# An expert stage on one core: experts written out in place of a loop, a token gather that serves two experts, 14 weight buffers in place of 12, and overflow blocks without a scatter of their own

## The chip, the cores and the metric

The kernel runs on one NeuronCore of a Trainium2 chip. The metric is the device time of one execution in microseconds. Before the change three runs took 2330.51, 2333.76 and 2336.15 us, median 2333.76.

## The reference

Two transformer blocks in fp32 for 256 tokens of width 1024. The part that the change touches is the mixture of experts in the first block:

```
logits = xt @ w_router + b_router                 # 256 x 32
top_logits, top_idx = top_k(logits, 4)            # 4 of 32 experts for each token
top_w = softmax(top_logits)
# for each expert e, over the tokens that chose it:
gate, up = split(xb @ w_gu[e] + b_gu[e], 2)       # w_gu[e]: 1024 x 2048
gate = minimum(gate, 7.0); up = clip(up, -7.0, 7.0)
act  = (up + 1) * (gate * sigmoid(1.702 * gate))
yb   = act @ w_dn[e] + b_dn[e]                    # w_dn[e]: 1024 x 1024
y[token] += yb * top_w
```

Each of the 32 experts has 12 MB of fp32 weights, 384 MB in all, read once. Before this stage comes a token mixer with its own projections, behind it pooling, a gated delta rule and two feed-forward layers; the change doesn't touch them.

## The kernel before

**Units.** All weights come in units of 1 MB, 128 partitions by 8 KB, issued in order by SyncE (SP). `ring` holds 10 of them; `area` is eleven slabs of 8 KB per partition for everything else. An expert is 12 units: 8 for gate and up (unit kt holds rows 128*kt and following of `w_gu`), 4 for the down projection (order `DN_ORDER`). In the expert stage unit u of every expert has the fixed buffer `eslot[u]` (line 184): the ring's 10 and the slabs 9 and 10. SP waits for `w_used`, which TensorE raises with the last matmul that reads a unit, and refills it (lines 506 to 515, one hardware loop over experts 1 to 31). TensorE waits for `w_full[u]` (line 986).

**Blocks.** Tokens of an expert are handled in blocks of 64 slots. An expert with over 64 tokens has overflow blocks (up to three) that run before its last block (`b` = 0) and read the same weights, without giving buffers back. `experts` (line 466) is the control flow of TensorE, VectorE and ScalarE alike: a hardware loop over the experts, in which the expert's token count is loaded into a register, then an inner hardware loop over b = 1 to 3 with an `If`: the overflow block, or an `Else` that only raises the step semaphore by the number of skipped steps (line 477). The three engines keep in step by counting semaphores (`Steps`, line 435): a wait names an expert, a block and a step.

**A last block on TensorE** (line 1066): bias matmuls for gate and up (`gate_and_up`, line 967, recorded at 971), 32 gate and up matmuls with 64 stationary columns (979), the scatter of the *previous* block's output into four PSUM banks (1023, recorded at 1027), the gather of the next expert's tokens (`gather`, 956, recorded at 960: one-hot matmuls of h2_tok with `slots`, 64 columns wide), two transposes each of the activation (994), the transpose of the spread matrix (1002), 16 down matmuls (1016). An fp32 matmul that isn't a transpose leaves two records and two weight loads. In one block there are 146 matmul records and 146 loads, 292.

**An overflow block** (line 1053): it waits until ScalarE has finished with the block before (`AC.started`), gathers its own tokens, waits for VectorE's copy of them, does gate and up, spread transpose, activation transposes and down, waits for ScalarE's y copy, and scatters its own output. It has buffers of its own for spread, spread_T and y (`spread_o`, `spread_T_o`, `y_blk_o`; `spread_o` lies in slab 5).

**VectorE** makes the one-hot masks (`find_slots`, line 1853, for the next expert; `find_spread`, 1860), the limits of gate and up (1872, 1873), the products (1877, 1881), the copies of the gathered tokens (1865) and of the transposed activation (1886). **ScalarE** does the sigmoid (1394), the copy of the transposed spread (1396) and, at a block's end, the copy of y out of PSUM (1401). Ahead of the loop TensorE gathers for expert 0 and starts the four output banks with the down bias (1049); VectorE makes the masks of expert 0 (1892) and copies g2 (1904) and the tokens (1906).

After the last expert the late stream of weights uses four ring buffers, which SP refills as expert 31 frees them (line 490), and ScalarE splits each unit in two parts (210).

## Time and profile before

| | |
|---|---|
| median of 3 runs | 2333.76 us (2330.51 to 2336.15) |
| the profiled execution | 2335.09 us |
| its span, first to last instruction | 2333.0 us |
| mean granted TensorE clock | 0.947 of 2.4 GHz |
| PE busy | 2102.5 us, 90% |
| PE weight loads | 1346.1 us, 58% |
| DVE busy | 854.8 us, 37% |
| ACT busy | 433.0 us, 19% |
| moved by DMA | 578.65 MB, mean 248 GB/s |

How to read it: PE is TensorE's matmuls and PEld its weight loads, DVE is VectorE, ACT ScalarE, SP SyncE. Times are us from the span's start unless marked ns. A line number is that of the kernel before. "Idle before" is the time in which the engine did nothing ahead of an instruction, with what ended it; "issue" is time for which the profile shows no cause, and PEq, ACTq and DVEq are sequencers. The DMA share is that of 16 DMA engines together; packets that overlap a little make a full load read as slightly over 100%. The expert stage begins near 400 us and ends near 1460 us.

### The profile page before, as it was taken

The numbers are of one execution on the slowest core, as the hardware profiler recorded it, in microseconds if no ns is written. First come the engines' busy times: TensorE is split into PE (matmuls) and PEld (weight loads), VectorE is DVE, ScalarE is ACT, GpSimd is POOL, SyncE is SP. The second block draws the span as 40 slices with busy tenths as digits, with TensorE's granted clock in tenths as the row PEclk, the third lists the DMA queues.
The fourth block names the chain that finished last, engine by engine and source line by source line (L and its number), as shares of the span: only waits on it lengthen the run. The fifth ranks groups of instructions, "written<-read, shape, count | busy, mean of one in ns | idle before, by whom it ended". The sixth has DMA issues, their size and how long they took to land. (4 is left out here: it accounts for less than half of the span.)

```text
span 2333.0 us, 30897 instructions
## 1 busy us (share of the span) xinstructions
PE 2102.5 (90%) x11317; PEld 1346.1 (58%) x11318; DVE 854.8 (37%) x1404; ACT 433.0 (19%) x503; POOL 61.8 (3%) x126
## 2 busy tenths in 40 slices
PE   5999996999999998999998989599988877769997
PEld 3768784434444443444443434389868865657986
DVE  1295335111111111111111111646557674544654
ACT  1011101001011000001100000135324422113541
POOL 2000002000000000000000000100000000000000
PEclk9999896999999999999999999799999986979999
DMA  9487322949999997999997948245554300124552
GB/s 362 159 285 277 121 108 92 401 192 419 422 422 422 422 422 329 368 422 422 422 422 317 385 194 356 100 156 186 189 166 142 108 1 1 55 65 138 181 198 73
DMA packets 142572, 578.65 MB, mean 248 GB/s; under 512 B 10521, under 2 KB 12041, under 8 KB 93259
## 3 DMA queue, kind: packets, MB, share of 16 engines
q1 hardware_dynamic: 135824, 563.12, 62.2%
q0 software_dynamic: 3552, 12.61, 1.6%
q10 hardware_dynamic: 3131, 1.98, 0.3%
q8 instruction: 50, 0.82, 0.1%
q14 instruction: 15, 0.12, 0.0%
HBM read 576.62 MB, written 1.05 MB: 248 GB/s over the span
## 5 line engine op out<-in xcount | busy, mean ns | idle before, releaser
L979 PE MATMUL bank<-ring,area 128*64 128x512 f32 x2304 | 505.6, 596 | 1.8 <-DMA ring<-in_w_gu 1.8
L979 PEld LDWEIGHTS bank<-ring,area 128*64 128x64 f32 x2304 | 167.3, 138 | 320.2 <-issue 306.8
L213 DVE TENSOR_TENSOR ring_r<-ring,ring_r 128x2048 fp32r<-128x2048 f32 x92 | 210.9, 2292 | 210.4 <-ACT ring_r L210 209.5
L709 PE MATMUL bank<-area,ring 128*128 128x256 f32 x1024 | 232.1, 390 | 9.9 <-issue 8.0
L709 PEld LDWEIGHTS bank<-area,ring 128*128 128x128 f32 x1024 | 200.3, 196 | 43.0 <-issue 12.1
L210 ACT ACTIVATE ring_r<-ring 128x2048 fp32r<-128x2048 f32 x92 | 175.8, 1912 | 234.6 <-PE bank L746 209.8
L1872 DVE TENSOR_SCALAR area<-bank 128x512 f32<-128x512 f32 x36 | 24.9, 691 | 505.1 <-PE bank L979 505.1
L743 PE MATMUL bank<-area_r,ring_r 128*128 128x256 f32 x704 | 201.4, 286 | 2.2 <-DVE area_r L1764 2.2
L745 PE MATMUL bank<-area_r,ring_r 128*128 128x256 f32 x704 | 200.1, 284 | 0.0
L746 PE MATMUL bank<-area_r,ring_r 128*128 128x256 f32 x704 | 200.0, 284 | 0.0
L743 PE MATMUL bank<-ring_r,area_r 128*128 128x512 f32 x384 | 153.2, 399 | 1.7 <-DVE area_r L1764 1.7
L960 PEld LDWEIGHTS bank<-area 128*128 128x128 f32 x1184 | 135.0, 192 | 31.8 <-DVE area L1873 24.3
L745 PE MATMUL bank<-ring_r,area_r 128*128 128x512 f32 x384 | 151.9, 396 | 0.0
L746 PE MATMUL bank<-ring_r,area_r 128*128 128x512 f32 x384 | 151.8, 395 | 0.0
L960 PE MATMUL bank<-area 128*128 128x64 f32 x1184 | 140.0, 276 | 3.8 <-ACT area L1401 2.8
L743 PEld LDWEIGHTS bank<-area_r,ring_r 128*128 128x128 f32 x704 | 136.1, 193 | 3.1 <-issue 3.1
L745 PEld LDWEIGHTS bank<-area_r,ring_r 128*128 128x128 f32 x704 | 136.1, 193 | 0.5 <-issue 0.5
L746 PEld LDWEIGHTS bank<-area_r,ring_r 128*128 128x128 f32 x704 | 136.1, 193 | 0.0
L1016 PE MATMUL bank<-ring,area 128*64 128x512 f32 x576 | 132.5, 602 | 0.6 <-DVE area L1886 0.5
L1016 PE MATMUL bank<-area 128*64 128x512 f32 x576 | 129.7, 592 | 0.0
L1394 ACT ACTIVATE area<-area 128x512 f32<-128x512 f32 x36 | 22.7, 629 | 456.9 <-DVE area L1872 456.9
L1853 DVE TENSOR_SCALAR area<-slot_row,place 128x64 f32<-128x64 f32 (+1 forms) x72 | 15.0, 251 | 234.6 <-PEq L477 231.5
(294 smaller groups left out, 1993.7 us busy)
## 6 DMA issues: line engine op xcount, KB each, us to landing
ring<-in_w_gu SPq DMA_DIRECT2D x256, 1024.0 KB, 15.8
ring<-in_w_dn SPq DMA_DIRECT2D x64, 1024.0 KB, 12.7
area<-in_w_dn SPq DMA_DIRECT2D x64, 1024.0 KB, 14.2
ring<-in_mlp_w SPq DMA_DIRECT2D x64, 1024.0 KB, 5.4
ring<-in_w_mod SPq DMA_DIRECT2D x24, 1024.0 KB, 7.5
ring<-in_w_in SPq DMA_DIRECT2D x24, 1024.0 KB, 9.1
ring<-in_gdn_w_in SPq DMA_DIRECT2D x16, 1024.0 KB, 5.4
ring<-in_ple_gate_w SPq DMA_DIRECT2D x8, 1024.0 KB, 7.5
```

Of the source, the lines that this page charges most:

```text
L210: nc.scalar.activation(unit_high(i), raw, ACT.Copy).then_inc(w_high, 1)
L213: nc.vector.tensor_tensor(unit_low(i), raw, unit_high(i), ALU.subtract).then_inc(w_split, 1)
L709: ins = mm(bank(g)[:, m * S:(m + 1) * S], u[k // UK][:, k % UK, c:c + P], xT[:, k, :], start=k == 0, stop=k == ND - 1)
L743: ins = mm(out_, a_[0], b_[0], start=start, stop=False)
L745: mm(out_, a_[0], b_[1], start=False, stop=False)
L746: return mm(out_, a_[1], b_[0], start=False, stop=stop)
L960: ins = mm(bX[:, d * BLK:(d + 1) * BLK], h2_tok[:, t, d * P:(d + 1) * P], s_[:, t, :], start=t == 0, stop=t == NT - 1)
L979: ins = mm(bk[hf * BLK:(hf + 1) * BLK, :], x[:, kt, :], eslot[kt][:, c:c + BANK], start=False, stop=kt == ND - 1)
L1016: ins = mm(bT[hf * BLK:(hf + 1) * BLK, :], actT[:, 2 * i + k, fh * BLK:(fh + 1) * BLK], eslot[u][:, c:c + BANK], start=n == 0 and k == 0, ...
L1394: f(g_sig, g_min, ACT.Sigmoid, scale=SWIGLU).then_inc(moe_act, 1)
L1853: step(v.tensor_scalar(dst[:, t, :], row, place[:, t, bass.ds(e, 1)], None, ALU.is_equal))
L1872: step(v.tensor_scalar(g_min, banks[5][:, :], LIMIT, None, ALU.min))
```

## The change

- The loop over experts is a Python loop: 32 copies of the inner loop and of the last block, on TensorE, VectorE, ScalarE and SP. The inner loop over overflow blocks stays a hardware loop in each copy. Waits in last blocks are on constants.
- `gather_pair` takes the place of `gather` for last blocks: the tokens of a pair of experts (128 columns) are gathered together, half of the features (4 of 8 slices) in each of the two blocks of the pair before. `slots` and `xg` have two halves; masks are made three experts ahead. The first pair is gathered ahead of the stage in two banks. Overflow blocks keep `gather`.
- 14 buffers: the ring's 10, slabs 9, 10, 5 and 8. Unit n of the 384 goes to buffer n mod 14.
- An overflow block no longer scatters its own output: like a last block it scatters that of the block before it, between gate/up and the transposes, and leaves its own to the next. It uses the shared spread, spread_T and y buffers, and waits for the y copy of the block before only there. The bias matmuls stand ahead of the wait for the token copy.

```
-        eslot = [ring[:, u, :, :].rearrange("p k n -> p (k n)") if u < RING else a(9 + u - RING)
-                 for u in range(NU)]
+        eslot = [ring[:, u, :, :].rearrange("p k n -> p (k n)") for u in range(RING)] + [a(9), a(10), a(5), a(8)]
+        ER = len(eslot)
+        def expert_slot(e, u):
+            return (NU * e + u) % ER
...
         def experts(eng, steps, overflow, last_block):
-            with eng.Fori(0, NE) as e:
-                n_tok = eng.value_load(counts[0:1, bass.ds(e, 1)], min_val=0, max_val=S)
+            for e in range(NE):
+                n_tok = eng.value_load(counts[0:1, e:e + 1], min_val=0, max_val=S)
                 with eng.Fori(1, NBLK) as b:
                     with eng.If(n_tok - b * BLK > 0):
                         overflow((e, b))
...
-            with sp.Fori(1, NE) as e:
+            for e in range(NE):
                 for u in range(NU):
-                    sp.wait_ge(w_used, e * NU + (PRE - NU + u + 1))
-                    sp.dma_start(eslot[u], expert_source(u, e)).then_inc(w_full[u], 16)
+                    n, s = NU * e + u, expert_slot(e, u)
+                    if n >= ER:
+                        sp.wait_ge(w_used, PRE + n - ER + 1)
+                    elif n < RING:
+                        sp.wait_ge(w_used, PRE - RING + n + 1)
+                    elif n == RING:
+                        sp.wait_ge(areas_free, 1)
+                    elif n == RING + 2:
+                        sp.wait_ge(w_used, PRE)
+                    elif n == RING + 3:
+                        full(sp, G("g2_bc", 1))
+                    sp.dma_start(eslot[s], expert_source(u, e)).then_inc(w_full[s], 16)
...
+            def gather_pair(bk, p, dh):
+                for d in range(UK):
+                    for t in range(NT):
+                        ins = mm(bk[:, d * P:(d + 1) * P], h2_tok[:, t, (UK * dh + d) * P:(UK * dh + d + 1) * P],
+                                 slots[:, p, t, :], start=t == 0, stop=t == NT - 1)
+                step(ins)
...
             def overflow(w):
                 DV.did(pe, w, "slots1")
-                AC.started(pe, w)
+                AC.started(pe, w, less=1)
                 gather(slots_o)
+                gate_up_bias()
                 DV.did(pe, w, "tokens")
-                gate_and_up(w[0], xg_o, False)
-                spread_transposed(w, spread_o)
+                gate_and_up(w, xg_o, False)
+                AC.started(pe, w)
+                scatter(spread_T, y_blk)
+                spread_transposed(w, spread)
                 activation_T(w, 0, bG)
                 activation_T(w, 1, bU)
                 down(w, False)
-                AC.did(pe, w, "down")
-                scatter(spread_T_o, y_blk_o)
...
             def last_block(w):
-                e = w[0]
+                pair, j = w[0] // 2, w[0] % 2
                 DV.started(pe, w)
-                gate_and_up(e, xg, True)
+                gate_up_bias()
+                gate_and_up(w, xg[:, pair % 2, :, j * BLK:(j + 1) * BLK], True)
                 AC.started(pe, w)
                 scatter(spread_T, y_blk).then_inc(w_used, 1)
                 DV.did(pe, w, "next_slots1")
-                gather(slots)
+                gather_pair(bX, (pair + 1) % 2, j)
...
-            for t in range(NT):
-                n[0] += 1
-                v.tensor_scalar(slots[:, t, :], slot_row[:, 0, 0, :], place[:, t, 0:1], None, ALU.is_equal)\
-                    .then_inc(dve_step, 1)
+            for e in range(3):
+                for t in range(NT):
+                    n[0] += 1
+                    v.tensor_scalar(slots[:, e // 2, t, e % 2 * BLK:(e % 2 + 1) * BLK], slot_row[:, 0, 0, :],
+                                    place[:, t, e:e + 1], None, ALU.is_equal).then_inc(dve_step, 1)
```

## Rows read from the trace of the kernel before

**Rows 1.** Timeline: first gate matmul, y copies of ScalarE (start, us, engine, line)

```profile
402.95 16.54 PE L979 MATMUL bank<-ring,area 128*64 128x512 f32 x64
...
492.38 0.60 ACT L1401 ACTIVATE area<-bank 128x512 f32<-128x512 f32 x1 [9.12 <-PE bank L1016]
...
553.47 0.60 ACT L1401 ACTIVATE area<-bank 128x512 f32<-128x512 f32 x1 [6.64 <-PE bank L1016]
...
838.12 0.60 ACT L1401 ACTIVATE area<-bank 128x512 f32<-128x512 f32 x1 [6.64 <-PE bank L1016]
...
897.77 0.60 ACT L1401 ACTIVATE area<-bank 128x512 f32<-128x512 f32 x1 [6.64 <-PE bank L1016]
...
1247.12 0.60 ACT L1401 ACTIVATE area<-bank 128x512 f32<-128x512 f32 x1 [6.64 <-PE bank L1016]
...
1277.50 0.60 ACT L1401 ACTIVATE area<-bank 128x512 f32<-128x512 f32 x1 [9.12 <-PE bank L1016]
...
1459.69 0.60 ACT L1401 ACTIVATE area<-bank 128x512 f32<-128x512 f32 x1 [6.64 <-PE bank L1016]
```

**Rows 2.** Windows: length, five engines' busy (x), clock, DMA share, GB/s

```profile
450.00:500.00 50.00, 43.34 (x234) 19.66 (x236) 8.40 (x23) 5.05 (x7) 0.00 (x0) 1.00 0.42 175
550.00:600.00 50.00, 49.33 (x254) 20.09 (x250) 8.79 (x22) 5.40 (x7) 0.00 (x0) 1.00 1.01 422
```

**Rows 3.** Who waited for whom, loads of TensorE, stage (us, times, longest)

```profile
PEld bank L979 <- DMA ring<-in_w_gu: 7.2, 8, 1.4
```

**Rows 4.** The timeline of one plain block and the next one's start

```profile
712.10 3.79 PE L960 MATMUL bank<-area 128*128 128x64 f32 x32
712.41 0.76 DVE L1881 SCALAR_TENSOR_TENSOR area<-area 128x256 f32<-128x256 f32 x2
...
724.25 0.60 ACT L1401 ACTIVATE area<-bank 128x512 f32<-128x512 f32 x1 [6.64 <-PE bank L1016]
...
724.83 5.75 PE L979 MATMUL bank<-ring,area 128*64 128x512 f32 x26
...
727.38 1.28 ACT L1394 ACT_TABLE_LOAD   x1 [2.54 <-ACTq L477]
```

**Rows 5.** The timeline of TensorE behind the stage, matmuls 128x128 by 128

```profile
1480.06 0.39 PE L1096 MATMUL bank<-apad,area 128*128 128x128 f32 x2
1480.28 0.39 PE L1098 MATMUL bank<-apad,area 128*128 128x128 f32 x2
```

**Rows 6.** The timeline of TensorE, overflow block of expert 2 and the block after

```profile
462.66 3.79 PE L960 MATMUL bank<-area 128*128 128x64 f32 x32 [0.70 <-ACT area L1401]
...
484.23 0.84 PE L994 MATMUL bank<-ident,area 128*128 128x128 f32 x4 [2.28 <-DVE area L1881]
...
497.15 3.18 PE L979 MATMUL bank<-ring,area 128*64 128x512 f32 x14
```

**Rows 7.** The timeline ahead of the stage

```profile
390.68 0.42 DVE L1892 TENSOR_SCALAR area<-slot_row,place 128x64 f32<-128x64 f32 x2
...
402.09 0.19 PEld L971 LDWEIGHTS bank<-area,expert_sel 96*64 96x64 bf16 x4 [4.24 <-DVE area L1853]
```

**Rows 8.** Queue q8: whole page, then 410 to 1450; a window between two packets

```profile
q8 instruction: 50, 0.82, 0.1%
...
q8 instruction: 1, 0.02, 0.0%
...
1561.17:1576.40 15.23, 15.23 (x130) 1.00 0.64 199
```

**Rows 9.** Queues at 162.3:163.6, 163.6:164.9, 164.9:166.2 (packets, MB, share of 16 engines)

```profile
q1 hardware_dynamic: 264, 0.51, 106.6%
...
q1 hardware_dynamic: 237, 0.49, 99.2%
q8 instruction: 1, 0.02, 5.3%
...
q1 hardware_dynamic: 258, 0.50, 104.6%
```

More of the change, by code:

```diff
@@ L323, in empties @@
             ins.then_inc(bank_free[g % BANKS], 1)
-        w_full = [sem(f"w_full{u}") for u in range(NU)]
+        w_full = [sem(f"w_full{u}") for u in range(ER)]
         w_used = sem("w_used")
@@ L961, in gather, with gate_up_bias @@
                                  start=t == 0, stop=t == NT - 1)
-                        if d == 0 and t == 0:
-                            first = ins
                 step(ins)
-                return first
-            def gate_and_up(e, x, last):
+            def gate_up_bias():
                 for part, bk in ((0, bG), (1, bU)):
@@ L1016, in down @@
                             ins = mm(bT[hf * BLK:(hf + 1) * BLK, :], actT[:, 2 * i + k, fh * BLK:(fh + 1) * BLK],
[L1017 removed]
+                                     block_u[:, c:c + BANK], start=n == 0 and k == 0, stop=n == 3 and k == 1)
                     if last:
@@ L1037, in _ @@
             pe.wait_ge(moe_dve, 1)
+            assert all(G("g2_bc", q) % BANKS not in (4, 6) for q in range(2)) and G("gateT") % BANKS not in (4, 6)
+            for dh in range(2):
+                gather_pair((bX, bU)[dh], 0, dh)
+            emptied(pe, G("gateT"))
             for q in range(2):
-                if G("g2_bc", q) % BANKS == 4:
-                    emptied(pe, G("g2_bc", q))
-            gather(slots)
-            emptied(pe, G("gateT"))
+                emptied(pe, G("g2_bc", q))
             pe.wait_ge(route_ready, 4)
             pe.wait_ge(bgu_ready, 1)
-            for q in range(2):
-                emptied(pe, G("g2_bc", q))
             for i in range(4):
@@ L1072, in last_block @@
                 DV.did(pe, w, "next_slots1")
-                gather(slots)
+                gather_pair(bX, (pair + 1) % 2, j)
                 activation_T(w, 0, bG)
```

90 lines of the change are left out of this document (46 added, 44 removed).

## The prediction

> **What bounds the kernel now.** I read the page's slices first, then windows of the expert stage, then the marks that each block leaves on ScalarE, then single blocks, then who waits for what, and last the instruction queue. The profiled execution took 2335.09 us with a span of 2333.0 us, 1.3 us over the median of 2333.76. The expert stage is 45% of it: from the first gate matmul at 402.95 us to the last y copy at 1459.69 us, 1056.7 us [rows 1]. The transfers run at 422 GB/s with all 16 engines full where no overflow block is near (550 to 600), and at 175 GB/s around the first one, where every buffer is full [rows 2]. TensorE's clock is 1.00 in the full stretches, the upper level of 2.4 GHz.
>
> An expert's 12 units are 12.58 MB: at 422 GB/s 29.8 us, 2.486 us for a unit. TensorE needs less: the marks of ten experts in a row (553.47 to 838.12) are 28.46 us apart, and only then come two at 29.8 (to 897.77), the pace of the transfers [rows 1]. So TensorE eats up the lead of 12 buffers at 1.4 us an expert; just as it is gone the next overflow block comes, in which TensorE frees no buffer for 30 us. Waits of the gate matmuls for weights come to only 7.2 us on the load side [rows 3]. **The two limits lie 5% apart**: whatever is saved on TensorE in the long runs (experts 2 to 15 and 16 to 26) can only reach the transfers' limit. Overflow blocks belong to experts 2, 16, 27 and 29: a mark with an idle of 9 us or more ends one.
>
> **Part by part.**
>
> *Gather for two.* Today one block gathers 64 slots with 32 matmul records in 3.79 us, between the scatter and the transposes, on the path [rows 4]. That is 0.118 us a record though only 64 columns move. The new half gather has 16 records with 128 moving columns. Such matmuls stand in L1096 and L1098: a pair starts every 0.22 us, 0.11 us for one [rows 5]. 16 of them are 1.8 to 1.9 us. The saving lies between nothing and 2.0 us; I take 1.95, as those rows are the same shape back to back. Does the gate chain still hide? SCALAR_TENSOR_TENSOR ends at 713.17; scatter and short gather end at 714.0, so the transposes don't wait; the token copy, 128x512 as before, follows the gather by the same 0.3 us. TensorE's pace becomes 28.46 - 1.95 = **26.5 us**.
>
> *Overflow blocks.* Before, one waits 0.70 us for the y copy before it gathers [rows 6]; and the block after it starts its gate 4.8 us after the down projection (own scatter 1.99, y copy, masks, turn of the loop) where a plain one needs 0.6: 492.38 to 497.15 against 724.25 to 724.83 [rows 1, 4, 6]. Now the scatter lies where the gate chain left TensorE idle for 2.28 us. The bias matmuls go under the token copy (0.6). The block takes 29.7 in place of 30.4, the next loses 4.2.
>
> *14 buffers.* The two more are filled before the stage, when the queue is idle, and let the transfers run 5.0 us longer at each stop. SP's queue is passed in order: unit 12 needs only the last earlier use, unit 13 the copy of g2, which VectorE makes right behind the masks of [rows 7], 10 us before the stage; nothing urgent stands behind them. At the other end the late stream's first four units take the buffers of expert 31's units 6 to 9 rather than 0 to 3, some 12 us later; the last comes free 4 us before the end and is needed after it, so I put nothing on it. If that cover fails, ScalarE's first splits slip by up to 2 us.
>
> *Head.* Four more mask instructions of 0.21 us stand before the first gather: +0.8 us, on the path [rows 7].
>
> *Waits on constants.* ScalarE's turn between blocks idles 2.54 us before its table load [rows 4]; TensorE's turn is hidden but for 0.2 us behind queued matmuls. Constants spare a few register steps of it; nothing.
>
> *Written out 32 times.* This is the part with a price that one must look for. A block body is 292 TensorE records, and the loop has two bodies. In the whole stage the instruction queue q8 fetches one packet of 16 KB: the loop stays resident. Outside it fetches one per 130 matmuls with their 130 loads, 50 in all [rows 8]. Written out, an expert is 260 + 292 records (the overflow body is passed over but lies there), 552, and with control some 575: 2.25 packets each, 70 more in the stage. What does one cost? In three windows of 1.3 us at full load the weights' queue q1 has 106.6%, 99.2% and 104.6% of 16 engines, and in the middle one q8 has 5.3%: 0.053 x 16 x 1.3 = 1.10 us of an engine, taken from q1 one for one [rows 9]. A unit is spread over all 16 engines and has landed when the last has its share. If q8 always sits on **one and the same engine**, that engine serves 29.83 + 2.25 x 1.10 to 1.2 = 32.4 us per expert and everyone waits for it: a unit takes 2.70 us. If the packets spread, or slip between, it stays 2.486. No row of the kernel before decides this. All 50 packets come one at a time from one queue of one sequencer; q1 has its packets on 16 engines at once. I take one engine.
>
> **The sum**, in stretches between the marks (before; then with a unit at 2.70; then at 2.486):
> - Experts 0 and 1 and the overflow of 2: 89.4; 89.4 - 3.9 + 0.8 - 0.7 = 85.6; 85.6.
> - Experts 2 to 15: 405.4. All 14 buffers are full, 168 - 14 = 154 units come, plus 4 us to start after the standstill and 2 us to use the last: 421.8; 388.8. TensorE alone would need 371.
> - Overflow of 16 and experts 16 to 26: 349.4. The overflow waits for its own weights, 31.5; 29.7. Some 11.8 units come meanwhile, 120.2 are left, plus 2: 326.8; 300.6. So 358.3; 330.3.
> - Overflow of 27: 30.4; 31.5; 29.7.
> - Experts 27 to 31 with the overflow of 29: 182.2; 5 x 26.5 + 29.7 = 162.2; 162.2.
>
> Together 1056.7; 1059.4; 996.6. So +2.7 us with one engine, -60 without. The 23 us saved in the short stretches and at the overflow blocks are given back in the two long ones.
>
> To both comes the jump over the overflow body, 303 instructions, more than one packet: where its target isn't there TensorE stands still. In the long runs the transfers hide it; 11 jumps are unhidden. Price: at least the packet's 1.1 us, at most the 4.2 us that the loads idle at the loop's first entry [rows 7]; with a quarter to all of them late this is 3 to 46 us. I take 2.7 us on a quarter: 7 us.
>
> Forecast: 2335.1 + 2.7 + 7 - 1.3 (to the median) = **2344 us**.
>
> **Rivals.**
> - *The fetches cost nothing* (the other side: faster). 2335.1 - 60 + 7 - 1.3 = 2281 us. Point of decision: fetch time per expert on the fullest engine; below 1.5 us an expert (a unit at 2.61) the kernel gains over 15 us, at 2.4 it is level. For it: that a queue may use many engines, as q1 does. Against: the one-for-one loss at full load. The Trainium skill (Runtime: NRT & Kernel Launch, section Instruction fetch mechanics) says that crossing a fetch boundary is "mostly hidden"; by that rule this rival is what happens. It speaks of the sequencer, and of that the rows agree: no matmul gap stands at a packet in straight code.
> - *Every jump is late.* TensorE's pace is 29.5 instead of 26.5 where it counts, 11 x 3 = 33 us more in place of 7: 2370 us. For it: the body passed over is longer than a packet, and the 4.24 us of idle at the loop's entry. Against: ScalarE's plain turn also takes 2.54 us, so most of that can be control alone. The same section says that a taken branch out of the resident window stalls for a fetch, and that kernels prefer full unrolling for it; here the branch stays when the loop goes, so the rule would turn against this change.
> - *The half gather is no shorter* (bound of that term). Pace 28.46: 14 us more with one engine, 2358 us; 36 more with spread fetches, 2318.
>
> **How the numbers follow.** One engine pays 0.58 (2344, own range 2328 to 2362), fetches free 0.29 (2270 to 2318), late jumps 0.13. The range 2282 to 2362 leaves out the lower part of the free case and most of the late jumps. About 0.2%, 4.7 us, is what a measurement can tell. The first case lies 10 us over the kernel before with some 10 us of doubt: 0.08 of it faster, 0.20 same. So faster 0.34, same 0.12, slower 0.54.
>
> **What would show it.** Marks in experts 3 to 6 at 26.5 us (gather right), at 28.5 (not). Marks in 9 to 15 at 32.4 (one engine) or 29.8 (free), and GB/s there 388 or 422. q8: about 70 packets more. q1's share of 16 engines there well below 100% with waits of TensorE for the ring (one engine), or at 101% (free). Idle of 1 to 4 us before L971's loads on some experts: late jumps. Overflow blocks 29.7 us. I am wrong altogether if the late stage after 1460 moves by more than 2 us by itself.

## The result and the profile after

The changed kernel takes **2315.57 us** (median of 4 runs, 2312.82 to 2318.56) against 2333.99 for the kernel before beside it: ratio 0.9918, 95% interval 0.9901 to 0.9936. It is 18 us faster, 0.8%. The forecast was 2344 us, slower: the sign is wrong, the range of 2282 to 2362 us holds the time.

The profiled execution took 2318.56 us, span 2316.8 us. First the marks (the y copy that ScalarE makes at a block's end, now L1424) that answer to [rows 1]: ends of expert 1, of 2's overflow block, of experts 2, 3, 4 and 15, of 16's overflow block, of 26, of 27's overflow block and of 31.

```profile
460.70 0.60 ACT L1424 ACTIVATE area<-bank 128x512 f32<-128x512 f32 x1 [6.71 <-PE bank L1038]
489.90 0.60 ACT L1424 ACTIVATE area<-bank 128x512 f32<-128x512 f32 x1 [8.09 <-PE bank L1038]
517.98 0.60 ACT L1424 ACTIVATE area<-bank 128x512 f32<-128x512 f32 x1 [6.71 <-PE bank L1038]
544.35 0.60 ACT L1424 ACTIVATE area<-bank 128x512 f32<-128x512 f32 x1 [6.71 <-PE bank L1038]
579.00 0.60 ACT L1424 ACTIVATE area<-bank 128x512 f32<-128x512 f32 x1 [6.71 <-PE bank L1038]
...
895.24 0.60 ACT L1424 ACTIVATE area<-bank 128x512 f32<-128x512 f32 x1 [6.71 <-PE bank L1038]
924.44 0.60 ACT L1424 ACTIVATE area<-bank 128x512 f32<-128x512 f32 x1 [8.09 <-PE bank L1038]
...
1238.42 0.60 ACT L1424 ACTIVATE area<-bank 128x512 f32<-128x512 f32 x1 [6.71 <-PE bank L1038]
1267.62 0.60 ACT L1424 ACTIVATE area<-bank 128x512 f32<-128x512 f32 x1 [8.09 <-PE bank L1038]
...
1442.95 0.60 ACT L1424 ACTIVATE area<-bank 128x512 f32<-128x512 f32 x1 [6.71 <-PE bank L1038]
```

The expert stage, from the first gate matmul at 403.56 to the last mark, is 1039.4 us (before 1056.7). What follows the last mark is the same: 873.9 against 873.3 us. A clean block takes 544.35 - 517.98 = 26.37 us, an overflow block 29.20. But every fourth expert takes 33.4 to 34.7 us (579.00 - 544.35 = 34.65), and the one after it often 28 to 30. The timeline of TensorE at the first matmuls of blocks (bias, L989; experts 3, 4, 5, 6, 7 and 8) shows where that goes; the bracket is the idle time before them:

```profile
517.76 0.60 PE L989 MATMUL bank<-area,expert_sel 96*64 96x512 bf16 x4
549.55 1.06 PE L989 MATMUL bank<-area,expert_sel 96*64 96x512 bf16 x4 [5.25 <-DVE area L1876]
581.00 0.62 PE L989 MATMUL bank<-area,expert_sel 96*64 96x512 bf16 x4 [2.05 <-DVE area L1876]
609.02 0.62 PE L989 MATMUL bank<-area,expert_sel 96*64 96x512 bf16 x4 [1.46 <-DVE area L1876]
635.41 0.60 PE L989 MATMUL bank<-area,expert_sel 96*64 96x512 bf16 x4
667.33 1.06 PE L989 MATMUL bank<-area,expert_sel 96*64 96x512 bf16 x4 [5.39 <-DVE area L1876]
```

The releaser that is named, VectorE's mask, is a consequence and not the cause. At expert 4 that mask starts at 549.26 us, after 11.77 us in which VectorE waited for TensorE's sequencer (PEq L486, the count that TensorE raises behind its jump):

```profile
549.26 0.42 DVE L1876 TENSOR_SCALAR area<-slot_row,place 128x64 f32<-128x64 f32 x2 [11.77 <-PEq L486]
```

VectorE had raised the count for which TensorE's bias matmuls wait by 540.04. After 5.25 us of idle the four bias matmuls take 1.06 us in place of 0.62, and the next window has a lower clock. Windows at the stall (length, busy time of PE, PEld, DVE, ACT, POOL, granted clock, DMA share, GB/s):

```profile
540.00:550.00 10.00, 4.75 (x26) 1.38 (x22) 0.74 (x4) 0.60 (x1) 0.00 (x0) 0.92 1.01 416
550.00:560.00 10.00, 10.00 (x38) 3.26 (x36) 0.18 (x1) 0.00 (x0) 0.00 (x0) 0.73 0.98 398
560.00:570.00 10.00, 10.00 (x52) 4.10 (x49) 2.74 (x5) 0.63 (x1) 0.00 (x0) 1.00 0.97 393
```

So one stall costs its 5.25 us and 3 more, in which TensorE runs partly at 1.2 GHz. Against a plain 26.37 us (28.04 behind an overflow block) the blocks lose 70 us in all by the marks, 46 of them in six blocks that take 33.4 us or more.

Who waited for whom in the stage, on TensorE and its loads; no line of TensorE or of its loads names weights:

```profile
PEld bank L989 <- DVE area L1876: 73.5, 31, 6.3
PE bank L989 <- DVE area L1876: 55.0, 19, 5.4
```

And the queues in 500 to 900, where the transfers are full in both kernels, first before, then after (packets, MB, share of 16 engines):

```profile
q1 hardware_dynamic: 23003, 167.60, 100.9%
```

```profile
q1 hardware_dynamic: 22943, 167.05, 100.6%
q8 instruction: 31, 0.51, 0.5%
```

31 packets of code came in these 400 us, and q1 moved 0.55 MB less: just about the code's own bytes. **One engine always held up by q8 would have cost 31 x 1.1 = 34 us of 400, some 14 MB.** The reason that I gave for a unit of 2.70 us is refuted by this alone.

### The profile page after: what moved, and what is told of

It is laid out like the page before. It is cut to its first block and busy times, and to the rows that moved or that the text cites. A ratio compares the mean times of both kernels' runs of the same rounds, so it can differ in the third digit from the quotient of the medians.

```text
span 2316.8 us, 27597 instructions
## 1 busy us (share of the span) xinstructions
PE 2059.3 (89%) x10805; PEld 1299.8 (56%) x10805; DVE 856.3 (37%) x1408; ACT 388.4 (17%) x467; POOL 61.7 (3%) x126
## 5 line engine op out<-in xcount | busy, mean ns | idle before, releaser
L1000 PE MATMUL bank<-ring,area 128*64 128x512 f32 x1632 | 370.5, 609 | 0.7 <-issue 0.5
L1000 PEld LDWEIGHTS bank<-ring,area 128*64 128x64 f32 x1632 | 124.4, 141 | 232.8 <-issue 229.4
L1038 PE MATMUL bank<-ring,area 128*64 128x512 f32 x848 | 188.6, 595 | 0.5 <-DVE area L1909 0.5
L1000 PE MATMUL bank<-area 128*64 128x512 f32 x672 | 152.4, 603 | 2.0 <-issue 1.3
L1038 PEld LDWEIGHTS bank<-ring,area 128*64 128x64 f32 x848 | 58.5, 137 | 112.3 <-issue 104.8
L1000 PEld LDWEIGHTS bank<-area 128*64 128x64 f32 x672 | 50.9, 139 | 94.6 <-issue 91.0
```

The costliest lines, as they stand in the source:

```text
L1000: ins = mm(bk[hf * BLK:(hf + 1) * BLK, :], x[:, kt, :], block_u[:, c:c + BANK], start=False, stop=kt == ND - 1)
L1038: ins = mm(bT[hf * BLK:(hf + 1) * BLK, :], actT[:, 2 * i + k, fh * BLK:(fh + 1) * BLK], block_u[:, c:c + BANK], start=n == 0 and k == 0, s ...
```

## The experiments

Theories. **J**: TensorE stands still at the jump over the overflow body because the code behind it isn't there, and loses clock afterwards. **C**: the control instructions of the inner loop cost, whatever they jump over. **E**: fetches hold up one DMA engine. All times are medians; the kernel before, run beside them, was at 2333.96 to 2336.7. A stage's length is taken from the first gate matmul to the last mark of the profiled execution; a table below has them all.

### Taking the jump away, shortening it, doubling it

```diff
 # x1_no_jump, all three engines, 28 experts
+                if e not in OVER:                     # OVER = (2, 16, 27, 29)
+                    eng.wait_ge(steps.sem, steps.base + e * steps.per)
+                    eng.sem_inc(steps.sem, (NBLK - 1) * steps.over_len)
+                    last_block((e, 0))
+                    continue
 # x2_short_body, TensorE only, control kept
             def overflow(w):
+                if w[0] not in OVER:
+                    gate_up_bias()
+                    return
 # x3_double_body: in place of gate_up_bias() the body's matmuls twice
 # x4_before_written_out: the kernel before with
-            with eng.Fori(0, NE) as e:
+            for e in range(NE):
```

x1 leaves out the test of the token count and the overflow path of 28 experts; x2 and x3 have other code in those paths, which this data never takes. No other part of the computation is left out.

> The changed kernel, with the count, the inner loop and the overflow body left out on all three engines for the 28 experts that have no overflow block with these tokens (an input with other overflows is not handled). Theory J (the time lost against the sum is TensorE standing still at the jump over the overflow body, because the instructions behind it are not there yet, with a spell at the lower clock after each): no 5 us idle ahead of an expert's bias matmuls is left, marks 26.4 us apart until the lead is used and 29.9 after that, stage 1039 us -> about 997, total 2270 to 2280 us. Theory C (the lost time is the control code itself, count load and three turns): the same 2270 to 2280, so this run does not part J from C. Theory E (my prediction: q8 packets hold up one DMA engine): one packet per expert is left, a unit takes 2.486 + 0.1 = 2.58 us, stage about 1020, total about 2297, with waits of TensorE for the ring.

> The changed kernel with all of its control flow; only TensorE's overflow body of the 28 experts that never run it is cut from some 300 instructions to some 10. Theory J: the jump lands within the same or the next packet, as fast as without it, 2270 to 2285 us, marks 26.4. Theory C: nothing changes, 2316 us, marks of 33 to 34 every fourth expert stay. Theory E: as without the jump, about 2297.

> The changed kernel, TensorE's never-run overflow body written twice for the 28 experts, so that each jump passes over more than two packets of instructions. Theory J: every expert stands still for 5 us and loses 2 us more of clock, marks 33 to 34 for all, about 28 x 7 = 200 us in place of 77, total 2420 to 2450 us. Theory C: no change, 2316 us. Theory E: 3.4 packets per expert, 29.83 + 3.8 = 33.6 us per expert as the pace of the weights, total about 2390, and waits for the ring in place of idle ahead of the bias matmuls.

> The kernel before with nothing changed but the loops over experts written out on all engines (12 buffers, a gather for one, own scatter of the overflow blocks). Theory J: marks of 28.46 with 35 to 36 every fourth expert and some of 30, some 75 us lost, of which the transfers' slack gives nothing back: 2395 to 2410 us. Theory C: the turn gets no dearer by being written out, 2334 us. Theory E: between the two, 2350 to 2365 us, with waits for the ring.

Measured: x1 **2293.97** (ratio 0.9790, 0.9734 to 0.9846), x2 **2297.0** (0.9831, 0.9784 to 0.9878), x3 **2462.5** (1.0539, 1.0487 to 1.0591), x4 **2389.9** (1.0210, 1.0159 to 1.0260). x2 changed nothing but the length of code that TensorE never runs, and it took 19 us off, 29 us by the stage's length: J holds. C is out as the cause; what the control instructions do beside a wait is shown further below (x14). With the body doubled almost every block takes 34 us. The wait ahead of the bias matmuls, x3 in its stage:

```profile
PE bank L990 <- DVE area L1888: 130.7, 28, 6.3
```

In x1 and x2 it is gone, and weights bind instead; x2's longest waits of TensorE for weights:

```profile
PE bank L1001 <- DMA ring<-in_w_gu: 17.4, 33, 0.9
PE bank L1001 <- DMA area<-in_w_gu: 10.8, 20, 0.8
```

The forecasts of J missed, all the same. x1 and x2 came 14 and 12 us above their upper bounds, 2280 and 2285: their stages are 1009.7 and 1010.0 us long in place of 997, and 10 to 11 us more lie behind the stage (see below). x1's total is near what E had said (2297), but E had said it from a stage of 1020 us and a unit of 2.58 us, and the unit took 2.50 (next section). x3 is 12 us above its upper bound, and x4 5 us below its lower one.

x4 says what writing out costs when it comes alone: 55 us by the medians, 45 us in the stage (1102.0 against 1056.7); the rest lies behind it. The other parts of the change had to earn that back.

The trace also has the records of TensorE's sequencer (PEldq here). All branches at this line, shortest, median and longest in ns, first and last start, in the changed kernel:

```profile
L481 PEldq COMPARE_BRANCH  x100: 77/215/6128, 395.9 to 1412.6; - x100
```

The longest branch at each expert's jump, in us; a dash stands for less than 0.6, "ov" has an overflow block:

```
expert    1    2    3    4    5    6    7    8    9    10   11   12
after     2.7  ov   -    6.0  2.8  2.3  -    6.1  2.8  -    -    6.0
x2        -    ov   -    -    -    -    -    -    -    -    -    -
x3        5.7  ov   6.1  5.4  5.8  5.9  7.1  5.7  5.6  6.2  6.0  6.0
```

That is J seen directly: the branch itself takes 6 us, with one packet of q8 landing in it (expert 4: the branch from 540.81 to 546.80, the packet from 544.27 to 545.29).

### What a fetch does to the transfers

```diff
 # x5_pool_jumps: x1_no_jump, and on GpSimd
+            for e in range(2, 28):
+                pool.wait_ge(w_used, PRE + NU * e)
+                n_tok = pool.value_load(counts[0:1, e:e + 1], min_val=0, max_val=S)
+                for _ in range(3):
+                    with pool.If(n_tok - 2 * S > 0):
+                        for _ in range(560):
+                            pool.wait_ge(bgu_ready, 1)
```

> x1_no_jump, with 78 never-taken bodies of 560 waits added on GpSimd's instruction stream, three beside each of experts 2 to 27; GpSimd has nothing else to do in this stage, so only the fetches of its code are added, and the result is the reference's. x1 has the weights as its bound there (pace 29.8 us per expert from expert 9 on, 38 packets of 16 KB on q8). I expect at least one more packet per jump, so 116 or more on q8, perhaps twice that. Theory E (every fetch goes over one of the 16 DMA engines, the reason I gave in the prediction for a unit of 2.70 us): that engine needs 0.62 us for 16.4 KB where it moves 65.5 KB in a unit of 2.486 us, so 78 more packets cost about 48 us and 156 about 97 us, less some 30 us while the tensor engine is still the bound (experts 0 to 9): last mark 1411 -> 1430 to 1480, total 2294 -> 2315 to 2365. Theory S (fetches are spread over the engines, or small beside the rest): 0.04 us each, total within 6 us of x1's 2294.

Measured 2293.5 (0.9814, 0.9797 to 0.9830), as x1. But q8 has 38 packets in 400 to 1430 as in x1: none of the expected 78 shows on it. The run adds nothing for or against E, since nothing shows that GpSimd's code was fetched where I meant it to be. What counts against E are the two q1 lines above, and x1's own pace where weights bind: experts 9 to 15 take 210.3 us, 30.04 each with one packet per expert, where E would have 29.83 + 1.1 = 30.9. A packet isn't free there, though. The same experts take 29.84 each in x13, where no packet comes, and 30.04 in x7, with one; experts 10 to 15 of x11, with two, take 30.24. So where TensorE waits for each unit a packet goes with some 0.2 us, a fifth of what E had. These are four kernels side by side, and no run changed the packets alone.

### The parts of the change one by one

```diff
 # x8_after_gather_twice: the changed kernel; x6_no_jump_gather_twice: x1_no_jump
+                gather_pair(bX, (pair + 1) % 2, j)    # without its step
                 gather_pair(bX, (pair + 1) % 2, j)
 # x12_after_12: the changed kernel; x7_no_jump_12: x1_no_jump
-  + [a(9), a(10), a(5), a(8)]
+  + [a(9), a(10)]
```

> x1_no_jump with the half gather of each last block issued twice, so that a block has the matmuls of the whole gather again (16 more, 1.76 us by rows of before); the result is the reference's. Theory D (without the jump the weights' transfers bind, at 29.8 us per expert, and a block of the tensor engine is 26.37 us): blocks become 28.1 us, still under 29.8, so the first nine experts are slower but the end moves by 0 to 6 us: total 2294 to 2300. Rival P (the tensor engine still sets the end): 31 x 1.76 = 55 us more, total 2349.

> The changed kernel with the half gather of each last block issued twice (16 matmuls, 1.76 us a block); the result is the reference's. Theory J (in the changed kernel the tensor engine sets the end, since no matmul waits for weights and every fourth block loses 7 us at the jump): 31 x 1.76 = 55 us more, total 2370; the slower clock after a stall could add up to 5. Rival D (weights bind a good part of it): at most 30 us more, total 2345.

> x1_no_jump with 12 unit buffers, the two new ones taken away again. Theory D (transfers bind): two units of room less; the queue waits where an overflow block holds a unit or a block is slow, and what is lost there is not made up: 5 to 12 us more, total 2299 to 2306. Rival: buffers bring nothing, since the queue is always 12 deep: 0 to 2 us, total 2294.

> The changed kernel with 12 unit buffers. Since TensorE sets the end there and waits for no weights, two units of room less should show only where the transfers fall behind in the stretch of experts 2 to 15: 0 to 6 us more, total 2316 to 2322. Rival: the queue waits more often and the weights bind: up to 20 us more.

Measured: x8 **2375.6** (1.0154, 1.0125 to 1.0183), 60 us over the changed kernel: with the jumps in place TensorE sets the end everywhere, and each of 31 half gathers is worth about its full 1.78 us (clean blocks 28.15 against 26.37, 31 x 1.78 = 55). By the stage's length it is 49.9 us (1089.3 against 1039.4), with five jumps of 6 us in place of six; the other 11 us of its profiled execution lie behind the stage. x6 **2315.7** (0.9924, 0.9894 to 0.9953), 22 over x1 where I had expected 0 to 6. The marks show why: behind each overflow block the buffers are full, and for seven experts of x1 TensorE sets the pace even at 26.37, for up to thirteen of x6 at 28.15. x6's stage is 19.2 us longer (1028.9 against 1009.7), nearly the whole difference. (Its last mark, 1424.10 against 1411.38, comes only 12.7 us later, since its stage began 6.5 us earlier, at 395.18 against 401.69, behind the same work.) x12 **2320.2** (0.9941, 0.9921 to 0.9962), 5 over the changed kernel; x7 **2303.8** (0.9865, 0.9846 to 0.9883), 10 over x1. So the two buffers are worth 5 us as the change stands and 10 where weights bind more; 3.4 and 8.4 us by the stages.

### Why only every fourth expert

An expert is 583 TensorE instructions in the changed kernel, 305 of them jumped over (counted in the built program). Packets of q8 are 16.4 KB. From the runs so far I made a rule F: packets of 256 instructions counted from the last missed target, the next one asked for when the current one is entered. It gives misses at experts 4, 8, 12, 16, 20, 24 and 28 of the changed kernel, which is what the branches show but for 16, where an overflow block ran. Three kernels put it to the test, each with a forecast of its own.

```diff
 # x9_padded: an expert is 768 instructions, by a second body that is never run
+                with pe.If(n_tok_now[0] - (S - 1) > 0):
+                    for _ in range(360 if w[0] else 185):
+                        pe.wait_ge(moe_dve, 1)
                 gather_pair(bX, (pair + 1) % 2, j)
 # x10_place_free; x11_place_late has 81 in place of 124
             def overflow(w):
+                if w[0] not in (0,) + OVER:
+                    for _ in range(124 if w[0] == 1 else 116):
+                        mm(bG[0:BLK, :], expert_sel[:, :], bgu_parts[:, 0:BANK], start=True, stop=False)
+                    pe.wait_ge(moe_dve, 1)
+                    return
```

> The changed kernel with every path kept and the result the reference's; only a second never-taken body, 180 satisfied waits' worth of TensorE instructions, is put into the middle of each last block (ahead of the half gather), so that an expert takes 768 instructions of the program in place of 583. Theory F (what the runs so far suggest): TensorE's code comes in packets of 16.4 KB, which is 256 instructions; the packets are counted from the target of the last jump that missed, and the packet behind the current one is asked for when the current one is entered. A jump over 305 instructions lands one packet on, which is there, or two packets on, which is not: then TensorE stands for a fetch (5.3 us). In the changed kernel the place of the jump in its packet is 22, 93, 164 and 235 for four experts in turn; 235 + 305 lies two packets on, which gives the miss at experts 4, 8, 12, 16, 20, 24 and 28, and 22 is the 2 us wait of the expert after it. With 768 = 3 x 256 the place is the same for every expert (118), both jumps land one packet on: no miss, no 2 us waits, about 3 packets per expert on q8 (96 in place of 72), blocks of 26.37 us until the weights bind at 29.8, total that of x1_no_jump, 2294 within 10, and faster than the changed kernel by about 20. Rival G (any jump over much code costs, and more jumps cost more): slower than 2316, by a few us per expert if the second jump costs as the first, 2330 to 2400.

> The changed kernel with TensorE's never-run overflow bodies of 27 experts cut from 305 to about 234 instructions, so that an expert takes 512, and that of expert 1 a little longer than the others (by 86 instructions than in x11_place_late). The result is the reference's, since those bodies aren't run. Theory F: the jump's place in its packet is 96 to 108 for experts 3 to 15 and 157 to 166 for 17 to 27, always landing on the packet behind: no wait ahead of the bias matmuls, 26.37 us a block until the weights bind, last mark near 1411, total 2280 to 2300. Only expert 29 (place 226, body of full length) could miss.

> The same kernel as x10_place_free but for expert 1's never-run body, 86 instructions shorter, which shifts the place of all later jumps: 10 to 22 for experts 3 to 15 and 70 to 80 for 17 to 27. Theory F: right behind the start of a packet the next one has only just been asked for, so experts 3 to 15 each wait about 2 us, as experts 1, 5, 9 of the changed kernel do (blocks of 28.0 to 28.6 us in place of 26.37, seen in experts 3 to 8, before the weights bind), and 17 to 27 don't. Rival H (it is the length of the skipped body that costs, not its place): x10 and x11 show the same blocks throughout.

Measured: x9 **2360.1** (1.0108, 1.0087 to 1.0129), x10 **2305.9** (0.9880, 0.9845 to 0.9914), x11 **2298.0** (0.9846, 0.9808 to 0.9884). x9 was forecast at 2294 by F and lies in the range of rival G (2330 to 2400), though not by G's reason: the second jump of each expert never takes over 0.37 us, it is the first that now waits more often. Between x10 and x11 only expert 1's never-run body differs. Their totals, of two runs each, overlap (2301.2 and 2310.6; 2292.3 and 2303.7), but their blocks differ, which rules out H. TensorE at the starts of experts 5 to 8 of x10:

```profile
572.76 0.62 PE L990 MATMUL bank<-area,expert_sel 96*64 96x512 bf16 x4 [1.43 <-DVE area L1882]
600.46 0.62 PE L990 MATMUL bank<-area,expert_sel 96*64 96x512 bf16 x4 [1.15 <-DVE area L1882]
628.27 0.62 PE L990 MATMUL bank<-area,expert_sel 96*64 96x512 bf16 x4 [1.25 <-DVE area L1882]
656.16 0.62 PE L990 MATMUL bank<-area,expert_sel 96*64 96x512 bf16 x4 [1.34 <-DVE area L1882]
```

and of experts 5 to 8 of x11:

```profile
566.35 0.60 PE L990 MATMUL bank<-area,expert_sel 96*64 96x512 bf16 x4
593.48 0.60 PE L990 MATMUL bank<-area,expert_sel 96*64 96x512 bf16 x4
619.85 0.60 PE L990 MATMUL bank<-area,expert_sel 96*64 96x512 bf16 x4
646.22 0.60 PE L990 MATMUL bank<-area,expert_sel 96*64 96x512 bf16 x4
```

But it is x10's branches that wait and x11's that don't, the reverse of what F said. In one thing x11 went F's way: its experts 3, 4 and 5 take 27.9, 27.8 and 27.1 us, with the idle time not at the branch but a few matmuls behind it, in straight code, where a packet of q8 has only just landed (510.64 to 511.74). The start of expert 3 of x11:

```profile
510.70 0.60 PE L990 MATMUL bank<-area,expert_sel 96*64 96x512 bf16 x4
511.14 1.02 PE L1001 MATMUL bank<-ring,area 128*64 128x512 f32 x3
513.09 3.17 PE L1001 MATMUL bank<-ring,area 128*64 128x512 f32 x13 [0.93 <-issue]
```

The branches of experts 3 to 18:

```
expert    3    4    5    6    7    8    9    10   11   12   13   14   15   16   17   18
x9        -    -    2.0  2.3  2.2  2.0  2.5  2.6  6.0  2.5  2.7  5.6  2.8  ov   6.0  5.8
x10       -    -    2.2  1.9  2.0  2.1  2.3  2.6  2.6  2.8  2.8  2.7  -    ov   2.2  2.1
x11       -    -    -    -    -    -    -    -    -    -    -    -    -    ov   -    -
```

In x9 every expert but the first has the same length, and the waits still grow from none to 6 us within 17 experts; experts 19 to 23 wait 5.6 to 7.8 us, and from 24 on no branch takes 0.6 us again. At x9's expert 24, with no long branch, the sequencer stands from 1187.0 to 1192.5 us between two instructions just behind the branch, and TensorE idles 5.33 us as elsewhere: the wait is for code, at the branch or right behind it. **F is wrong in its details**: the place of the jump decides, but I can't compute it, and padding a program until its waits vanish isn't a cure. What stays shown is that a jump over 305 instructions waits for 0, for 2 to 3 or for about 6 us (7.8 once), that over 230 for at most 2.9, over 10 for nothing.

### The sequencer's lead, and versions that keep every path

```diff
 # x14_one_test: the changed kernel, all three engines
+                with eng.If(n_tok - BLK > 0):
                     with eng.Fori(1, NBLK) as b:
                         ...
+                with eng.Else():
+                    eng.wait_ge(steps.sem, e * steps.per + steps.base)
+                    eng.sem_inc(steps.sem, (NBLK - 1) * steps.over_len)
 # x13_loop: 12 buffers, fixed tiles, one loop body; x15_loop_one_test: both
-            for e in range(NE):
+            with eng.Fori(0, NE // 2) as p_:
+                with eng.Fori(0, 2) as j:
+                    e = p_ * 2 + j
 ...
+                with pe.If(now[1] > 0):
+                    gather_pair(bX, 1)
+                with pe.Else():
+                    gather_pair(bX, 0)
```

> The changed kernel with one test ahead of the loop over overflow blocks (more than 64 tokens or not) in place of three passes through the loop, on TensorE, VectorE and ScalarE; the result is the reference's. In the trace of the changed kernel TensorE's sequencer takes 4.0 us from loading the count to the last branch of the loop, and is that far ahead of the matmuls, so that a branch which waits 6.0 us for its target's code leaves TensorE idle for 5.3 us and one of 2.7 us for 2 us. Theory Q (the sequencer's lead is used up by its own 4 us there, so every wait of a branch is felt): with one test those 4.0 become about 1.5 us; the 6 us waits remain at every fourth expert and leave 2.8 us idle in place of 5.3, the 2.7 us waits leave none. 7 x 2.5 + 8 x 1.8 = 32 us less, a little more by the clock, up to where the weights bind: total 2285 to 2300. Rival R (the lead isn't there; the wait is felt whatever stands beside it): total 2316 as the changed kernel, idle times unchanged.

> The changed kernel's gather for two and its overflow block, but with the experts in hardware loops again (16 pairs, 2 experts in a pair) as in the kernel before, and 12 unit buffers. Which half is gathered is chosen by a test of the inner loop's variable on TensorE and VectorE, and VectorE copies the block's tokens to one fixed place (3 small copies more, 2 of the slot masks more). The result is the reference's. The loop is about 640 instructions of TensorE in place of 32 x 583. Theory F (code that has been run is still there, and only code that comes anew must be fetched): no fetch in the loop (1 or 2 packets on q8 between 410 and 1400, as in the kernel before), all jumps short, blocks of 26.4 to 26.8 us until the weights bind at 29.8, total as x7_no_jump_12, 2304 within 8. Rival J2 (a jump over 305 instructions costs by itself, loop or not): 5 us a block where nothing hides it, total 2340 or more.

> x13_loop with the one test of x14_one_test. Where the weights bind, nothing more is to be had: total as x13_loop within 5 (2300). If x13_loop is slower because of the jump (rival J2), this one shows no gain on it under R and 2.5 us an expert under Q.

Measured: x14 **2296.95** (0.9851, 0.9830 to 0.9872), x13 **2309.4** (0.9888, 0.9857 to 0.9919), x15 **2307.7** (0.9891, 0.9874 to 0.9907). All three keep every path.

In x14 the branches still take 6.0 to 6.2 us at eight experts and 2.2 to 3.1 at seven others, but TensorE idles 2.5 to 2.9 us at the first and not at all at the second. The blocks of experts 6 to 11; now the profile names the sequencer itself:

```profile
591.31 0.60 PE L993 MATMUL bank<-area,expert_sel 96*64 96x512 bf16 x4
617.67 0.60 PE L993 MATMUL bank<-area,expert_sel 96*64 96x512 bf16 x4
647.97 0.62 PE L993 MATMUL bank<-area,expert_sel 96*64 96x512 bf16 x4 [2.60 <-PEq L490]
674.36 0.60 PE L993 MATMUL bank<-area,expert_sel 96*64 96x512 bf16 x4
700.73 0.60 PE L993 MATMUL bank<-area,expert_sel 96*64 96x512 bf16 x4
733.87 0.62 PE L993 MATMUL bank<-area,expert_sel 96*64 96x512 bf16 x4 [2.88 <-PEq L490]
```

```profile
PE bank L993 <- PEq L490: 21.6, 8, 2.9
```

At five of these eight stalls the clock stays: expert 4's block takes 29.14 us, 2.8 us over the clean 26.37, with 2.6 of idle. Behind the other three (experts 15, 19 and 22, idle 2.5 to 2.8 us) the granted clock falls for a few us, and these blocks take 30.6 to 31.1 us. The window at expert 15:

```profile
855.00:865.00 10.00, 10.00 (x42) 3.82 (x40) 0.50 (x2) 0.00 (x0) 0.00 (x0) 0.83 1.02 422
```

So a stall of 2.5 to 2.9 us costs 3 to 5 us, one of 5.3 cost 8. That is theory Q. At expert 4 of the changed kernel the sequencer loads the count at 539.86 us and the matmuls before it end at 544.30, so it is 4.4 us ahead. Its three passes through the empty loop take 4.0 of these (513.49 to 517.44 at expert 3), and nearly the whole branch wait is felt. In x14 the count and the one test take 1.25 us, and 3 us of the wait stay hidden.

In x13 and x15 q8 shows one packet in 410 to 1400, as in the kernel before, and no branch behind the loop's first takes 0.6 us:

```profile
q8 instruction: 1, 0.02, 0.0%
```

So J2 is out: a jump over 305 instructions costs nothing where the code at its target has been run before, one expert earlier. (The 305 themselves need not have been: at expert 1 they hadn't.) x13's blocks take 26.8 to 27.3 us, x15's 26.38. Their stages, 1020.6 and 1021.8 us, are as long as that of x7 (1018.1), which has 12 buffers too, and 2 to 3 us longer than x14's 1018.4. Most of what they are behind x14 in the total, 11 to 12 us, lies behind the stage.

### What lies behind the stage

The time from the last mark to the end isn't always the 873 us of the kernel before and after. Stage and rest of the profiled executions, in us:

| kernel | stage | behind it |
|---|---|---|
| before | 1056.7 | 873.3 |
| after | 1039.4 | 873.9 |
| x1 | 1009.7 | 884.7 |
| x2 | 1010.0 | 883.5 |
| x3 | 1186.1 | 873.4 |
| x4 | 1102.0 | 884.9 |
| x5 | 1007.6 | 894.7 |
| x6 | 1028.9 | 883.6 |
| x7 | 1018.1 | 880.9 |
| x8 | 1089.3 | 884.8 |
| x9 | 1075.1 | 890.2 |
| x10 | 1022.0 | 872.9 |
| x11 | 1018.9 | 873.1 |
| x12 | 1042.8 | 873.0 |
| x13 | 1020.6 | 889.4 |
| x14 | 1018.4 | 873.7 |
| x15 | 1021.8 | 883.8 |

It goes with the clock. Windows of 10 us that begin 20 and 30 us behind the last mark, changed kernel, then x1:

```profile
1462.95:1472.95 10.00, 9.15 (x48) 6.49 (x48) 4.17 (x4) 2.39 (x4) 1.07 (x2) 0.98 0.30 105
1472.95:1482.95 10.00, 7.60 (x28) 4.29 (x27) 4.81 (x9) 0.00 (x0) 0.00 (x0) 1.00 0.00 0
```

```profile
1431.38:1441.38 10.00, 7.08 (x30) 4.72 (x29) 3.48 (x3) 1.99 (x4) 1.07 (x2) 0.76 0.28 105
1441.38:1451.38 10.00, 10.00 (x21) 5.42 (x20) 1.98 (x3) 0.00 (x0) 0.00 (x0) 0.50 0.00 0
```

TensorE has the same work there and is granted 2.4 GHz in one and 1.2 in the other; in x1 the lower level lasts until 73 us behind the last mark. One of x1's four runs took 2274.8 and one of x4's 2375.4 us, 14 to 23 below their others, so I read this as a matter of where the end of the stage falls. No run was made to steer it, and it stays open. It blurs comparisons of totals by 10 to 20 us; stages are compared by their length here for that reason. It hides a part of what x1 gains over the changed kernel (29.7 us in the stage, 21.6 in the total), and it makes x4 and x8 look 10 us dearer than their stages are. The start of the stage moves as well, from 395.2 us (x6) to 404.5 us (x10), where the changed kernel has 403.56 and x1 401.69.

## Why the prediction was wrong

By stretches of the stage, as the forecast had them ("one engine" and "free" are its two sums; x1 is the changed kernel without the jumps):

| stretch | before | one engine | free | after | x1 |
|---|---|---|---|---|---|
| experts 0, 1, overflow of 2 | 89.4 | 85.6 | 85.6 | 86.3 | 83.7 |
| experts 2 to 15 | 405.4 | 421.8 | 388.8 | 405.3 | 396.6 |
| overflow of 16, 16 to 26 | 349.4 | 358.3 | 330.3 | 343.2 | 335.7 |
| overflow of 27 | 30.4 | 31.5 | 29.7 | 29.2 | 29.2 |
| 27 to 31, overflow of 29 | 182.2 | 162.2 | 162.2 | 175.3 | 164.5 |
| together | 1056.7 | 1059.4 | 996.6 | 1039.4 | 1009.7 |

- **The step that failed first is "I take one engine".** It said that all packets go over one and the same DMA engine, so that a unit takes 2.70 us. Beside the fetches a unit takes 2.49 to 2.50 us, as the q1 lines and x1's pace show, and a packet goes with some 0.2 us in place of 1.1. I had one row with 5.3% of q8 and q1 down by as much, and read "which engine" out of the fact that packets come one at a time. That was an argument, not a row. It put 63 us more than the free sum on the long stretches and the overflow block of 27, some 50 more than x1 measured there.
- **The second is the price of the jump**, 2.7 us on a quarter of 11 jumps, 7 us. The share was too low: six of 28 jumps wait 6 us, near the quarter, but eight more wait 1.9 to 2.8. The size was too: 5.3 us idle and up to 3 of clock for the first, and in all 28 blocks 70 us of TensorE's time. "In the long runs the transfers hide it" was wrong as well: the stalls raise the mean block of four experts to 29.2 us, just under the 29.8 of the weights, so in the changed kernel TensorE waits for no weights at all and every stall counts until the pace reaches the transfers'. Net the jumps cost 1039.4 - 1009.7 = 29.7 us of the stage. I had bounded the price by 1.1 us, the packet's time on an engine, and by the 4.24 us that the loads idle in [rows 7]; the 5.3 us lie above both. The trace of the kernel before had a row that I didn't read, TensorE's sequencer at this jump. Its longest branch, 3.4 us, is the loop's first, from 395.13 to 398.55 us. It ends as that idle time has just begun, and the three passes through the inner loop fill the rest; in the stage none takes over 0.25 us:

```profile
L472 PEldq COMPARE_BRANCH  x100: 77/208/3427, 395.1 to 1430.4; - x100
```

- I didn't price the clock. Each of the six stalls of 5.2 to 5.4 us took TensorE to 1.2 GHz for a few us, but some shorter ones did too: those of 2.0 and 1.9 us at experts 9 and 13, whose blocks took 30.2 us, and three of x14's. Others of that length didn't. What decides it stays open.
- **The free ledger was 13 us short** (996.6 against x1's 1009.7), 8 of it in experts 2 to 15. Part of it is the 0.2 us with each packet; the rest I can only put on the terms of start and end of a stretch, 4 and 2 us, and no run took them apart.
- **That the range held the time is luck.** 2344 less 63 for the engine, plus 13 for the free ledger and 23 for the jumps (30 in place of 7), is 2317, near the 2315.6 measured: the misses went opposite ways. The range of the case that I chose, 2328 to 2362 us, missed.
- Right: the clean block, 26.5 forecast and 26.37 measured; the half gather at 0.11 us a record (x8: 1.78 us); the overflow block, 29.7 and 29.20; q8, 70 packets more in the stage and 71 seen. The clean block has a part that I had put at nothing: written out alone it takes 28.10 us (x4) in place of 28.46, so 0.36 us come from writing out and 1.73 from the gather, which I had at 1.95. The head, +0.8 forecast and +0.6 seen, and the late stage, unmoved at +0.6 us, agree for this pair of profiles only, since the head moves by up to 9 us and the late stage by up to 21 between kernels with the same work there.
- By its mechanism, what came nearest is *fetches cost nothing* for the transfers together with *every jump late* for TensorE: 2281 + 26 = 2307, a case that I never summed since I had them as alternatives. They act on different engines, and both can be true. (The sum nearest in number, 2318 for a half gather no shorter with spread fetches, is so by luck: the gather was shorter.) The Trainium skill (Runtime: NRT & Kernel Launch, section Instruction fetch mechanics) says that crossing a fetch boundary is mostly hidden and that a taken branch whose target isn't resident waits for a fetch. The traces agree: in x1 and x2 no gap for code shows in straight code, and the branch waits 6.0 us here. Right behind a jump straight code waits as well in x11 and x9. The preference for full unrolling that the Trainium skill has there doesn't hold for this kernel, where the branch stays: x4's stage is 45 us longer by it.

The stage got 17.3 us shorter. By the stages' lengths writing out alone costs 45 (x4), the gather for two brings 50 back on a kernel with jumps (x8), the buffers 3.4 (x12), and some 9 us remain for the overflow blocks, which no run took alone. By the marks they should bring more. One with its successor took 30.4 + 32.7 us before and takes 29.2 + 28.1 now, 23 us for all four, of which 7 are the half gather. The parts don't add up exactly, since the waits at jumps fall differently in each kernel.

## What to carry to other kernels

Written out code that keeps a rarely taken branch should keep the body behind it short, or stay a loop. A forward jump over more than about a packet of code to a target that has never been run can cost 6 us each time, and the profile puts it down to an innocent semaphore; the sequencer's own records, or the same idle time at every n-th copy, give it away. Take needless control steps off the sequencer just ahead of such a jump: x14, with one `If` around a loop, takes 2297 us and beats both kernels. And where two prices of an unknown act on different engines, sum them together before calling them rivals.

## What the runs showed of the hardware

- A branch of TensorE's sequencer to code that isn't there takes about 6 us while the weights stream at 420 GB/s (5.4 to 6.4 us in most cases, up to 7.8), against 0.08 to 0.44 us where the target is there.
- 31 packets of 16.4 KB in 400 us took 0.55 MB from the other transfers, about their own 0.51 MB. Where TensorE waited for each unit, an expert took 29.84 us without a packet (x13), 30.04 with one (x1, x7) and 30.24 with two (x11).
- The length of code that is never run changes the time: 2297 us, 2316 us and 2462 us for bodies of 10, 305 and twice as many instructions.
- A loop of 640 TensorE instructions, run 32 times over 1000 us, fetches one packet (x13).
- TensorE at 1.2 GHz: after an idle of 5.25 us the granted clock of the next 10 us was 0.73; after eight of 2.5 to 2.9 us it stayed at 1.00 five times and fell three times (x14).
